# Adding the experts' outputs to token rows in DRAM, block by block, instead of gathering them after the last block

## The chip, the cores and the metric

The kernel runs on one core of one Trainium2 chip. The metric is the device time of one execution in microseconds. Five engines work side by side, each through its own list of instructions: TensorE (PE in the profile; PEld is its weight load), VectorE (DVE), ScalarE (ACT), GpSimd (POOL) and SyncE (SP). They meet through semaphores only. Transfers are issued by SP, ACT or POOL and carried out by 16 DMA engines that all of them share.

## The reference

The program is one step of a two-layer decoder trunk over 576 tokens (512 prompt tokens and 64 sample tokens), width 1024, float32. Each layer mixes tokens by three kinds of heads and then has a feed-forward part. That of layer 0 is dense; that of layer 1, to which the change belongs, is a mixture of 8 experts of which each token uses 2. Then comes the final norm:

```
def moe(x):
    logits = xf @ moe_router                      # 8 experts
    top_v, top_i = lax.top_k(logits, 2)
    gw = softmax(top_v)
    comb = sum(one_hot(top_i, 8) * gw[..., None], axis=1)
    for e in range(8):
        y = y + comb[:, e:e+1] * ((silu(xf @ w1[e]) * (xf @ w3[e])) @ w2[e])    # 1024 -> 1408 -> 1024
    return y

x = x + moe(rmsnorm(x, norm_ffn_w))
y = x * rsqrt(mean(x * x) + 1e-6) * norm_final_w
```

The whole step returns y for both groups of tokens and the new caches and states of the two layers.

## The kernel before, in words

Everything up to layer 1's experts keeps the activations with channels on the 128 partitions. For the experts this turns round: tokens lie on partitions, in five tiles (four of 128 tokens, one of 64), and `XT` (`xt_buf`) holds the rows of x before the experts, 1024 numbers a token.

**Routing.** DVE finds each token's two experts (`moe_choose_dve`). A token and one of its experts are a pair, and there are 1152 of them. Pairs of one expert get consecutive slots, and each expert's slots begin at a multiple of 128, so that 16 blocks (`NBK`) of 128 slots always do. PE sums over the tokens with two small products (`moe_count_pe`); DVE turns the sums into a slot for each pair (`slot_buf`), an expert for each block (`ebt_buf`) and a weight for each pair (`gain`). POOL then writes the normed rows to their slots in `d_xs` in DRAM with ten indirect transfers, two for each tile (`moe_scatter_pool`, L2248). Slots without a token hold zeros, which layer 0 wrote there in its feed-forward part (`ex_sp`).

**Blocks.** For each of the 16 blocks SP loads the block's 128 rows and the expert's weights, in 18 units of up to 1 MB, into a ring of 11 slots (`moe_sp`, L2308). It issues a unit as soon as PE is done with the one 11 places ahead. ACT casts each unit to the high half of a split product (L2412), up to four units ahead of PE. DVE computes the low half (L2456) and PE multiplies (L2334, L2338 up; L2365, L2371 down). The output of a block, 128 slots by 1024, stands in PSUM banks 6 and 7. ACT copies it to `yb_buf` (L2436) and issues its transfer to `d_ys` in DRAM (L2438).

**After the last block.** When all of `d_ys` is written, POOL gathers for every tile the rows of its tokens' two slots (`moe_gather_pool`, L2260, ten indirect transfers through two buffers). DVE adds them to XT, each times its weight (L2504 twice a tile), ACT squares and sums (L2518), DVE scales the mean (L2507), ACT takes the root (L2520), DVE the reciprocal (L2509) and the product with the norm's weights (L2510), and SP stores the tile (L2860). The order of all engines is the order of the code; `v(...)` and `a(...)` are a helper (L165) that makes an engine wait for each of its own instructions. In `fin_dve` the next tile's additions come after this tile's last product.

Of the kernel before, what the change touches and what calls it, by code (L numbers as in the profile page):

```python
# [8 lines left out]
I32 = mybir.dt.int32  # L9
# [178 lines left out]
def build(nc, A):  # L188

    with ExitStack() as ctx:  # L190
        sems = {}
        A["xs"] = nc.dram_tensor("d_xs", (NBK * P, D), F32).ap()
        A["ys"] = nc.dram_tensor("d_ys", (NBK * P, D), F32).ap()
# [84 lines left out]
        yg_buf = put_at("yg_buf", 4 * D, mc + 9216)  # L278
# [1806 lines left out]
        YG = yg_buf[:, :].rearrange("p (i c d) -> p i c d", i=2, c=2)  # L2085
# [26 lines left out]
        frs = rt.take(5)  # L2112

# [276 lines left out]
        def moe_act():  # L2390
# [29 lines left out]
            for b in range(NBK):  # L2420
# [76 lines left out]
        def fin_dve(v):  # L2497
            ve = nc.vector
            ve.wait_ge(S("moe_wfin"), 16)
            for i in range(5):  # L2500
                n = tok(i)
                ve.wait_ge(S(f"moe_yg_{i % 2}"), 32 * (i // 2 + 1))
                for k in range(2):
                    v(ve.scalar_tensor_tensor(XT[0:n, i, :], YG[0:n, i % 2, k, :], gain[0:n, k, i:i + 1], XT[0:n, i, :],  # L2504
                                              ALU.mult, ALU.add), *([S("moe_added")] if k else []))
                ve.wait_ge(S("moe_fsum"), i + 1)
                v(ve.tensor_scalar(frs[0:n, i:i + 1], fsum[0:n, i:i + 1], 1.0 / D, 1e-6, ALU.mult, ALU.add), S("moe_fmean"))  # L2507
                ve.wait_ge(S("moe_froot"), i + 1)
                v(ve.reciprocal(frs[0:n, i:i + 1], frs[0:n, i:i + 1]))  # L2509
                v(ve.scalar_tensor_tensor(XT[0:n, i, :], XT[0:n, i, :], frs[0:n, i:i + 1], WFIN[0:n, :], ALU.mult, ALU.mult),  # L2510
                  S("moe_fin"))

        def fin_act(a):
            ac = nc.scalar
            for i in range(5):
                n = tok(i)
                ac.wait_ge(S("moe_added"), i + 1)
                a(ac.activation(sq_buf[0:n, 0:D], XT[0:n, i, :], ACT.Square, accum_out=fsum[0:n, i:i + 1]), S("moe_fsum"))  # L2518
                ac.wait_ge(S("moe_fmean"), i + 1)
                a(ac.activation(frs[0:n, i:i + 1], frs[0:n, i:i + 1], ACT.Sqrt), S("moe_froot"))  # L2520
# [9 lines left out]
        def ex_sp(e):  # L2530
            for u in range(NUN):
# [99 lines left out]
        with nc.Block() as block:  # L2631
            @block.vector
            def _(eng):
# [20 lines left out]
                for l in range(DEPTH):  # L2654
# [77 lines left out]
            def _(eng):  # L2732
                for l in range(DEPTH):
# [9 lines left out]
                    else:  # L2743
                        moe_scatter_pool()
                        moe_gather_pool()

            @block.tensor
            def _(eng):
                eng.wait_ge(S("g_consts"), 16)
                eng.sem_inc(S("ex_unit_done"), FREE_PARTS)  # L2750
                for l in range(DEPTH):
# [23 lines left out]
                    else:  # L2775
                        moe_wo_pe()
                        moe_count_pe()
                        moe_pe()

            @block.sync  # L2780
            def _(eng):
# [4 lines left out]
                for l in range(DEPTH):  # L2786
# [63 lines left out]
                    if l == 0:  # L2850
# [3 lines left out]
                        eng.wait_ge(S("g_zero"), 16 * NBK)  # L2854
# [188 lines left out]
```

## Time and profile before

| | us |
|---|---|
| median of 3 runs | 2856.9 |
| lowest and highest run | 2844.24, 2858.02 |
| span of the profiled execution | 2850.7 |

The page gives no time of its own for the profiled execution beside its span. Its part on busy shares shows PE busy for 2468.7 us (87%), DVE for 1668.5 (59%), ACT for 1125.7 (39%) and POOL for 360.3 (13%). In the 40 equal slices of the span PE stands at 9 tenths from slice 30 to slice 39, which are the blocks, and DMA there too. PE stands at 3 in the last slice, in which the gathers and the final norm lie. A span runs from the first to the last instruction; a stretch in which PE has nothing to do is time that only the other engines and the transfers can shorten.

### The profile page before, as it was taken

Reading aid. Unit: us, or ns where it says so; the run is one execution under the profiler, and the core shown is the slowest. Engines: PE = TensorE matmul, PEld = TensorE weight load, DVE = VectorE, ACT = ScalarE, POOL = GpSimd, SP = SyncE. Lnnn points to the kernel's source line nnn. Section 1 sums busy time; section 2 is a strip of 40 time slices with the busy share of each in tenths; the row PEclk is TensorE's granted clock in tenths of the full one; section 3 lists DMA queues with packets and bytes.
Section 4 is the critical chain, followed back from the end, with each engine's and each line's share of the span. In section 5 each row is a group of like instructions: output and inputs, shape, how many; then the busy total and the mean of one; then the engine's idle time right before and its main releaser. Section 6 shows DMA issues by size and latency. Waiting matters only on the chain.

```text
span 2850.7 us, 39807 instructions
## 1 busy us (share of the span) xinstructions
PE 2468.7 (87%) x15802; PEld 2095.7 (74%) x15802; DVE 1668.5 (59%) x1990; ACT 1125.7 (39%) x1370; POOL 360.3 (13%) x160
## 2 busy tenths in 40 slices
PE   5996798698779999969977886979599999999993
PEld 5995686334779999969965863349488888888883
DVE  6853765524423122158627655243689898989895
ACT  4441000453222112134420004532577777777773
POOL 2330000000133333313310000002100000000001
PEclk9997888696889999989978986969799999999997
DMA  4220311300022343122203113001799999999993
GB/s 150 78 61 16 127 53 51 121 23 30 31 96 87 106 149 110 61 94 78 69 16 127 53 51 123 22 30 38 309 420 401 380 381 383 381 387 379 384 376 113
DMA packets 115995, 452.28 MB, mean 159 GB/s; under 512 B 12834, under 2 KB 47522, under 8 KB 86370
## 3 DMA queue, kind: packets, MB, share of 16 engines
q1 hardware_dynamic: 110882, 431.92, 41.3%
q0 software_dynamic: 2624, 9.44, 1.0%
q10 hardware_dynamic: 2304, 8.39, 0.7%
q8 instruction: 125, 2.05, 0.3%
q14 instruction: 60, 0.49, 0.1%
HBM read 415.00 MB, written 42.95 MB: 161 GB/s over the span
## 4 chain that ended last, share of the span: by engine, by line
PE 78%; DVE 12%; ACT 4%; issue 2%; DMA 2%; POOL 1%; another core or an unknown queue 1%; DVEq 0%; SPq 0%; ACTq 0%; POOLq 0%; PEldq 0%
PE ps_buf L508 31%; PE ps_buf L2334 12%; PE ps_buf L2338 6%; PE ps_buf L2365 6%; PE ps_buf L1161 3%; PE ps_buf L2371 3%; PE ps_buf L1196 2%; ACT arena L1735 2%; PE ps_buf L1651 2%; PE ps_buf L1685 1%; PE ps_buf L1149 1%; PE ps_buf L1838 1%; DVE h_buf L572 1%; PE ps_buf L2349 1%; DVE xl_buf L576 1%
## 5 line engine op out<-in xcount | busy, mean ns | idle before, releaser
L508 PE MATMUL ps_buf<-xh_buf,whl_buf 128*128 128x288 f32 x3648 | 663.2, 302 | 76.6 <-POOLq L165 40.5
L2456 DVE TENSOR_TENSOR ring_lo<-ring,high_buf 128x2048 fp32r<-128x2048 f32 (+2 forms) x288 | 594.4, 2108 | 51.7 <-ACT high_buf L2412 49.5
L508 PEld LDWEIGHTS ps_buf<-xh_buf,whl_buf 128*128 128x128 f32 x3648 | 549.6, 192 | 89.5 <-issue 65.0
L2412 ACT CAST high_buf<-ring 128x2048 fp32r<-128x2048 f32 (+2 forms) x288 | 503.0, 1764 | 127.2 <-PE ps_buf L2338 69.0
L508 PE MATMUL ps_buf<-xl_buf,whl_buf 128*128 128x288 f32 x1824 | 398.4, 300 | 0.0
L496 POOL TENSOR_TENSOR whl_buf<-arena,whl_buf 128x1024 fp32r<-128x1024 f32 (+1 forms) x114 | 294.1, 2579 | 602.1 <-ACTq L165 601.5
L493 ACT CAST whl_buf<-arena 128x1024 fp32r<-128x1024 f32 (+1 forms) x114 | 124.7, 1094 | 495.5 <-PE ps_buf L508 476.2
L508 PEld LDWEIGHTS ps_buf<-xl_buf,whl_buf 128*128 128x128 f32 x1824 | 299.0, 193 | 0.0
L2334 PE MATMUL ps_buf<-high_buf,xbh_buf 128*128 128x512 f32 (+1 forms) x768 | 289.8, 377 | 5.3 <-ACT high_buf L2412 5.3
L2334 PE MATMUL ps_buf<-high_buf,xbl_buf 128*128 128x512 f32 (+1 forms) x768 | 288.3, 375 | 0.0
L2338 PE MATMUL ps_buf<-ring_lo,xbh_buf 128*128 128x512 f32 (+1 forms) x768 | 196.1, 377 | 0.0
L2365 PE MATMUL ps_buf<-high_buf,ht_buf 128*128 128x512 f32 x704 | 181.2, 397 | 0.0
L496 POOL TENSOR_TENSOR whl_buf<-cols_buf,whl_buf 128x1024 fp32r<-128x1024 f32 x16 | 39.7, 2479 | 1005.3 <-ACTq L165 1004.9
L2334 PEld LDWEIGHTS ps_buf<-high_buf,xbh_buf 128*128 128x128 f32 x768 | 144.8, 189 | 28.6 <-issue 5.7
L2334 PEld LDWEIGHTS ps_buf<-high_buf,xbl_buf 128*128 128x128 f32 x768 | 144.7, 188 | 23.0
L2338 PEld LDWEIGHTS ps_buf<-ring_lo,xbh_buf 128*128 128x128 f32 x768 | 140.6, 188 | 24.8 <-DVE ring_lo L2456 3.3
L2365 PEld LDWEIGHTS ps_buf<-high_buf,ht_buf 128*128 128x128 f32 x704 | 129.8, 188 | 28.4
L2584 DVE TENSOR_TENSOR cols_buf<-arena,ps_buf 128x576 f32<-128x576 f32 x22 | 16.6, 755 | 212.2 <-PE ps_buf L508 212.2
L508 PE MATMUL ps_buf<-hh_buf,whl_buf 128*128 128x288 f32 x704 | 122.9, 296 | 0.0
L2260 POOL DMA_INDIRECT yg_buf<-d_ys,slot_buf x10 | 9.4, 936 | 805.5 <-DMA d_ys<-yb_buf 789.9
L508 PEld LDWEIGHTS ps_buf<-hh_buf,whl_buf 128*128 128x128 f32 x704 | 103.5, 188 | 0.0
L2371 PE MATMUL ps_buf<-ring_lo,ht_buf 128*128 128x512 f32 x352 | 97.7, 396 | 0.0
(519 smaller groups left out, 3395.8 us busy)
## 6 DMA issues: line engine op xcount, KB each, us to landing
ring<-d_moe_up SPq DMA_DIRECT2D x128, 1024.0 KB, 7.5
ring<-d_moe_dn SPq DMA_DIRECT2D x80, 1024.0 KB, 7.4
ring<-d_moe_up SPq DMA_DIRECT2D x64, 768.0 KB, 6.6
arena<-d_w_in SPq DMA_DIRECT2D x54, 512.0 KB, 3.6
arena<-d_w SPq DMA_DIRECT2D x44, 512.0 KB, 3.6
arena<-d_w SPq DMA_DIRECT2D x16, 704.0 KB, 4.0
arena<-d_pages_c SPq DMA_DIRECT2D x64, 128.0 KB, 2.1
cols_buf<-d_w_out SPq DMA_DIRECT2D x16, 512.0 KB, 3.6
```

Of the source, the lines that this page charges most:

```text
L493: a(nc.scalar.copy(part(slot, 0, nk, size), src), *sig)
L496: g(nc.gpsimd.tensor_tensor(part(slot, 1, nk, size), src, part(slot, 0, nk, size).bitcast(F32), ALU.subtract), *sig)
L508: last = nc.tensor.matmul(ps_buf[0:rows, b + a_, 0:HALF], w, m[:, a_ * HALF:(a_ + 1) * HALF], start=start, stop=stop)
L1161: last = pe.matmul(ps_buf[0:n, 3 * s_ + b, c], l_[0:n, c], r_[0:n, c], start=True, stop=True)
L1196: last = nc.tensor.matmul(bank(4 * j + 2 * g + half, 9 * 32 + 8), cw1[j][:, 8 * half + p_, :], ckb[:, :, j, g, 8 * p_:8 * p_ + 8], start=p ...
L1651: pe.matmul(ps_buf[:, b + g, at:at + n], cols[lo:lo + 64, keys(w), P * c:P * c + P], qrot[lo:lo + 64, h, P * c:SEQ], start=True, stop=False)
L2334: pe.matmul(ps_buf[:, o + w, 0:n], x_[:, b % 2, 4 * q + k, :], high_part(u)[:, n * k:n * k + n], start=q == 0 and k == 0 and i == 0, stop= ...
L2338: last = pe.matmul(ps_buf[:, o + w, 0:n], XBH[:, b % 2, 4 * q + k, :], low_part(u)[:, n * k:n * k + n], start=False, stop=q == 1 and k == 3)
L2365: pe.matmul(ps_buf[:, 6 + h, 0:512], t_[:, f, :], high_part(u)[:, c], start=f == 0 and i == 0, stop=False)
L2371: last = pe.matmul(ps_buf[:, 6 + h, 0:512], HTH[:, f, :], low_part(u)[:, c], start=False, stop=f == FC - 1)
L2412: ac.copy(high_part(n), ring[:, 2048 * slot:2048 * slot + unit_cols(n % BLOCK_UNITS)])\
L2456: ve.tensor_tensor(low_part(n), ring[:, at:at + unit_cols(n % BLOCK_UNITS)], high_part(n).bitcast(F32), ALU.subtract).then_inc(S("moe_lo"), 1)
```

## The change

Each block's rows are multiplied by their slots' weights on the way out of PSUM, and added to their tokens' rows in DRAM at once.

- A new DRAM tensor `d_ya` of 704 rows takes the place of `d_ys`. SP copies XT into its rows 0 to 575 (five transfers) before the first block. Rows 576 to 703 take what slots without a token would add; they are zeroed once in layer 0.
- `moe_who_dve` and `moe_who_pe` compute, for each slot, its token's row (`who_buf`) and its weight (`share_buf`). DVE makes ten one-hot matrices, and PE sums ten small products into PSUM bank 2. Two more small products ahead of `moe_count_pe` give rows of numbers to compare with.
- ACT's copy of a block's output becomes a product with `share_buf`, and ACT issues no transfer any more. POOL issues an indirect transfer that adds (`moe_add_pool`), one for each block. Each waits for the block's output and for the addition before it. ACT waits for the addition of two blocks ago before it writes `yb_buf` again.
- After the last addition SP loads the five tiles of `d_ya` back into XT. `fin_dve` has no additions left, and the norm's steps of two tiles overlap: the mean of tile i stands ahead of the reciprocal and the product of tile i-1, and on ACT the squares of tile i stand ahead of the root of tile i-1. The table for the root is loaded ahead of the first tile.

```diff
-        A["ys"] = nc.dram_tensor("d_ys", (NBK * P, D), F32).ap()
+        A["ya"] = nc.dram_tensor("d_ya", (T + P, D), F32).ap()
...
+        def moe_who_dve(v):
+            ve = nc.vector
+            blk = tb("blocks")[:, ::8]
+            wide_b = blk.unsqueeze(1).to_broadcast([P, 10, NBK])
+            flat_s = slots.rearrange("p k i -> p (k i)")
+            v(ve.tensor_scalar(at_blk, flat_s, 1.0 / P, -1.0 / P, ALU.mult, ALU.add))
+            v(ve.tensor_tensor(eq, at_blk.unsqueeze(2).to_broadcast([P, 10, NBK]), wide_b, ALU.is_ge))
+            v(ve.tensor_reduce(at_blk, eq, AX.X, ALU.add))
+            v(ve.tensor_scalar(at_blk, at_blk, -1.0, None, ALU.add))
+            v(ve.tensor_tensor(eq, at_blk.unsqueeze(2).to_broadcast([P, 10, NBK]), wide_b, ALU.is_equal))
+            v(ve.scalar_tensor_tensor(at_blk, at_blk, -float(P), flat_s, ALU.mult, ALU.add))
+            v(ve.tensor_copy(number, ps_buf[:, 1, 128:129]))
+            v(ve.tensor_scalar(tok5, tb("steps")[:, ::8], number, None, ALU.add))
+            v(ve.tensor_scalar(number, number, float(T), None, ALU.add))
+            for k in range(2):
+                ks = slice(5 * k, 5 * k + 5)
+                v(ve.tensor_tensor(AG[:, ks, 0, :], eq[:, ks, :], tok5.unsqueeze(2).to_broadcast([P, 5, NBK]), ALU.mult))
+            v(ve.tensor_tensor(AG[:, :, 1, :], eq, gain.rearrange("p k i -> p (k i)").unsqueeze(2).to_broadcast([P, 10, NBK]),
+                               ALU.mult))
+            for j in range(10):
+                if j >= 2:
+                    ve.wait_ge(S("moe_whose"), j - 1)
+                v(ve.tensor_scalar(OH[:, j % 2, :], ps_buf[:, 1, 0:P], at_blk[:, j:j + 1], None, ALU.is_equal), S("moe_oh"))
+            ve.wait_ge(S("moe_whose"), 10)
+            v(ve.tensor_copy(share_buf[:, :], ps_buf[:, 2, NBK:2 * NBK]))
...
+            v(ve.tensor_scalar(who_buf[:, :], eq[:, 0, :], -1.0, None, ALU.add), S("moe_who"))
+
+        def moe_who_pe():
+            pe = nc.tensor
+            for j in range(10):
+                n = tok(j % 5)
+                pe.wait_ge(S("moe_oh"), j + 1)
+                pe.matmul(ps_buf[:, 2, 0:2 * NBK], OH[0:n, j % 2, :], AG[0:n, j].rearrange("p w b -> p (w b)"),
+                          start=j == 0, stop=j == 9).then_inc(S("moe_whose"), 1)
...
-        def moe_gather_pool():
...
+        def moe_add_pool():
+            g = nc.gpsimd
+            g.wait_ge(S("moe_ya"), 16 * 5)
+            g.wait_ge(S("moe_who"), 1)
+            for b in range(NBK):
+                g.wait_ge(S("moe_y"), b + 1)
+                if b:
+                    g.wait_ge(S("moe_acc"), 16 * b)
+                g.indirect_dma_start(A["ya"], bass.IndirectOffsetOnAxis(ap=who_buf[:, b:b + 1], axis=0), YB[:, b % 2, :], None,
+                                     compute_op=ALU.add).then_inc(S("moe_acc"), 16)
...
+            sp.wait_ge(S("moe_xt"), KD)
+            for i, (t0, n) in enumerate(TILES):
+                sp.dma_start(A["ya"][t0:t0 + n], XT[0:n, i, :]).then_inc(S("moe_ya"), 16)
             sp.wait_ge(S("moe_experts"), 1)
...
+                if b == 0:
+                    ac.wait_ge(S("moe_who"), 1)
                 if b >= 2:
-                    ac.wait_ge(S(f"moe_ys_{b % 2}"), 16 * (b // 2))
-                ac.copy(YB[:, b % 2, :].rearrange("p (h c) -> p h c", h=2), ps_buf[:, 6:8, 0:512]).then_inc(S("moe_y"), 1)
-                ac.wait_ge(S("moe_y"), b + 1)
-                ac.dma_start(A["ys"][P * b:P * b + P], YB[:, b % 2, :]).then_inc(S(f"moe_ys_{b % 2}"), 16)
+                    ac.wait_ge(S("moe_acc"), 16 * (b - 1))
+                ac.mul(YB[:, b % 2, :].rearrange("p (h c) -> p h c", h=2), ps_buf[:, 6:8, 0:512], share_buf[:, b:b + 1])\
+                    .then_inc(S("moe_y"), 1)
...
+            for i in range(6):
+                if i < 5:
+                    n = tok(i)
+                    ve.wait_ge(S("moe_fsum"), i + 1)
+                    v(ve.tensor_scalar(frs[0:n, i:i + 1], fsum[0:n, i:i + 1], 1.0 / D, 1e-6, ALU.mult, ALU.add), S("moe_fmean"))
+                if i:
+                    n = tok(i - 1)
+                    ve.wait_ge(S("moe_froot"), i)
+                    v(ve.reciprocal(frs[0:n, i - 1:i], frs[0:n, i - 1:i]))
+                    v(ve.scalar_tensor_tensor(XT[0:n, i - 1, :], XT[0:n, i - 1, :], frs[0:n, i - 1:i], WFIN[0:n, :],
+                                              ALU.mult, ALU.mult), S("moe_fin"))
...
+                eng.wait_ge(S("moe_acc"), 16 * NBK)
+                for i, (t0, n) in enumerate(TILES):
+                    eng.dma_start(XT[0:n, i, :], A["ya"][t0:t0 + n]).then_inc(S(f"moe_back_{i}"), 16)
```

How the instructions stand on an engine is shown here at three places, before and now. The line numbers are those of each kernel's own file, `part_...` and `ex_...` are semaphores that several stages share, and a row with xN stands for N alike.

POOL before, from the last scatters to the end: `d_xs` is the slots' input, `yg_buf` the gathered rows.

```order
L2248 DMA d_xs<-xn_tok,slot_buf 2048x1024 [waits part_75]
L2248 DMA d_xs<-xn_tok,slot_buf 2048x1024
L2260 DMA yg_buf<-d_ys,slot_buf 128x1024 [waits part_90,part_89]
L2260 DMA yg_buf<-d_ys,slot_buf 128x1024 x3
L2260 DMA yg_buf<-d_ys,slot_buf 128x1024 [waits part_54]
L2260 DMA yg_buf<-d_ys,slot_buf 128x1024
```

POOL now, the same place to the end of its list:

```order
L2296 DMA d_xs<-xn_tok,slot_buf 2048x1024 [waits part_75]
L2296 DMA d_xs<-xn_tok,slot_buf 2048x1024
L2307 DMA d_ya<-yb_buf,who_buf 704x1024 [waits part_88,ex_raw_in_0,part_97]
L2307 DMA d_ya<-yb_buf,who_buf 704x1024 [waits part_89,part_88] x15
L2686 UNCONDITIONAL_BRANCH
```

The ten gathers behind the blocks are gone; sixteen additions stand among the blocks, and the last of them behind the last block.

DVE now, between the routing and the first block (before, the product into `xbt_buf` followed at once on the third of these rows):

```order
L2238 TENSOR_SCALAR mo_buf<-mo_buf 128x5 [waits dve_chain,ex_silu]
L2239 RECIPROCAL mo_buf<-mo_buf 128x5 [waits dve_chain]
L2240 TENSOR_TENSOR mo_buf<-mo_buf 128x5 [waits dve_chain]
L2247 TENSOR_SCALAR mo_buf<-mo_buf 128x10 [waits dve_chain]
L2248 TENSOR_TENSOR mo_buf<-mo_buf,tab 128x160 [waits dve_chain]
L2249 TENSOR_REDUCE mo_buf<-mo_buf 128x10 [waits dve_chain]
```

and the end of the piece that is new there:

```order
L2264 TENSOR_SCALAR oh_buf<-ps_buf,mo_buf 128x128 [waits dve_chain] x2
L2264 TENSOR_SCALAR oh_buf<-ps_buf,mo_buf 128x128 [waits dve_chain,ex_raw_in_1] x8
L2266 COPY share_buf<-ps_buf 128x16 [waits dve_chain,ex_raw_in_1]
L2267 TENSOR_SCALAR mo_buf<-ps_buf,mo_buf 128x16 [waits dve_chain]
L2268 TENSOR_TENSOR mo_buf<-mo_buf,ps_buf 128x16 [waits dve_chain]
L2269 TENSOR_SCALAR who_buf<-mo_buf 128x16 [waits dve_chain]
L2498 TENSOR_TENSOR xbt_buf<-ps_buf,small 128x1024 [waits dve_chain,ex_raw_free]
```

Twenty-six instructions now stand ahead of the first block's product on DVE, eight of them with a wait for PE.

DVE before, in the final norm, the first tile and the start of the second:

```order
L2504 SCALAR_TENSOR_TENSOR xt_buf<-yg_buf,mo_buf,xt_buf 128x1024 [waits part_53,part_52]
L2504 SCALAR_TENSOR_TENSOR xt_buf<-yg_buf,mo_buf,xt_buf 128x1024 [waits dve_chain]
L2507 TENSOR_SCALAR mo_buf<-mo_buf 128x1 [waits dve_chain,part_55]
L2509 RECIPROCAL mo_buf<-mo_buf 128x1 [waits dve_chain,part_57]
L2510 SCALAR_TENSOR_TENSOR xt_buf<-xt_buf,mo_buf,wbc_buf 128x1024 [waits dve_chain]
L2504 SCALAR_TENSOR_TENSOR xt_buf<-yg_buf,mo_buf,xt_buf 128x1024 [waits dve_chain,part_59]
```

DVE now:

```order
L2554 TENSOR_SCALAR mo_buf<-mo_buf 128x1 [waits part_56,part_55]
L2554 TENSOR_SCALAR mo_buf<-mo_buf 128x1 [waits dve_chain,part_56]
L2558 RECIPROCAL mo_buf<-mo_buf 128x1 [waits dve_chain,part_58]
L2559 SCALAR_TENSOR_TENSOR xt_buf<-xt_buf,mo_buf,wbc_buf 128x1024 [waits dve_chain]
L2554 TENSOR_SCALAR mo_buf<-mo_buf 128x1 [waits dve_chain,part_56]
L2558 RECIPROCAL mo_buf<-mo_buf 128x1 [waits dve_chain,part_58]
```

The two additions of a tile are gone, and the mean of the next tile stands ahead of this tile's reciprocal.

## Rows read from the trace of the kernel before

**Rows 1.** The page: its first line.
```profile
span 2850.7 us, 39807 instructions
```

**Rows 2.** Busy time of each engine by stretch: two blocks and the end.
```profile
core 0: us, PE busy (x) PEld busy (x) DVE busy (x) ACT busy (x) POOL busy (x), PEclk, DMA share, GB/s
...
2083.00:2131.00 48.00, 48.00 (x230) 40.58 (x229) 43.36 (x27) 34.97 (x26) 0.00 (x0) 1.00 1.02 420
...
2276.00:2324.00 48.00, 48.00 (x230) 40.59 (x229) 43.30 (x28) 34.97 (x26) 0.00 (x0) 1.00 0.99 382
...
2805.00:2851.00 46.00, 0.00 (x0) 0.00 (x0) 20.82 (x25) 8.89 (x17) 9.36 (x10) 0.54 0.48 165
```

**Rows 3.** Waits from 2035 to 2805: total us, times, longest; SP's queue apart.
```profile
ACT high_buf L2412 <- DMA ring<-d_moe_up: 3.9, 6, 1.2
...
SPq L2308 <- PE ps_buf L2338: 382.3, 187, 6.0
SPq L2308 <- PE ps_buf L2371: 209.7, 90, 3.6
```

**Rows 4.** Transfers issued in 2083:2131 and then 2276:2324: count, KB, us to landing.
```profile
ring<-d_moe_up SPq DMA_DIRECT2D x8, 1024.0 KB, 13.0
...
ring<-d_moe_up SPq DMA_DIRECT2D x8, 1024.0 KB, 6.6
```

**Rows 5.** Chain that ended last, from 2803: start us, us, what.
```profile
2804.84 1.02 ACT yb_buf L2436
...
2808.50 0.74 issue
...
2810.52 5.37 DMA yg_buf<-d_ys,slot_buf
...
2829.23 1.29 DVE xt_buf L2504
...
2835.30 1.30 DVE xt_buf L2504
...
2846.00 1.28 DVE xt_buf L2510
```

**Rows 6.** Timeline of the third tile's norm: start us, us, instruction, idle before.
```profile
2831.92 1.06 ACT L2518 ACTIVATE sq_buf<-xt_buf 128x1024 f32<-128x1024 f32 x1 [4.40 <-DVEq L165]
...
2833.15 0.15 DVE L2507 TENSOR_SCALAR mo_buf<-mo_buf 128x1 f32<-128x1 f32 x1 [1.32 <-ACTq L165]
...
2833.39 0.20 ACT L2520 ACTIVATE mo_buf<-mo_buf 128x1 f32<-128x1 f32 x1 [0.32 <-DVEq L165]
2833.67 0.16 DVE L2509 RECIPROCAL mo_buf<-mo_buf 128x1 f32<-128x1 f32 x1 [0.37 <-ACTq L165]
2833.87 1.28 DVE L2510 SCALAR_TENSOR_TENSOR xt_buf<-xt_buf,mo_buf,wbc_buf 128x1024 f32<-128x1024 f32 x1
```

**Rows 7.** By tile, xn_tok: scatters, ACT's scaling, landing; then xb_buf's landing.
```profile
L2248 POOL DMA_INDIRECT d_xs<-xn_tok,slot_buf x10: 896/952/1132, 2007.0 to 2018.5; - x10
L2163 ACT ACTIVATE xn_tok<-xt_buf,mo_buf x5: 1147/1147/1148, 1999.1 to 2004.2; 128x1024 f32<-128x1024 f32 x4, 64x1024 f32<-64x1024 f32 x1
...
DMA to landing us min/median/max: 3.5/4.4/5.2
...
DMA to landing us min/median/max: 3.2/5.9/16.0
```

**Rows 8.** Chain from the routing to the first block, and two waits there.
```profile
2002.32 0.65 PE ps_buf L2237 x2
...
2003.43 0.21 DVE mo_buf L2208
...
2033.88 3.73 PE ps_buf L2334 x8
...
PE ps_buf L2317 <- DMA xb_buf<-d_xs: 23.2, 1, 23.2
DVE xbt_buf L2448 <- PE ps_buf L2317: 20.1, 1, 20.1
```

More of the change, by code:

```diff
@@ L277, in build @@
         xt_buf = put_at("xt_buf", 5 * D, mc + 4096)
-        yg_buf = put_at("yg_buf", 4 * D, mc + 9216)
+        who_buf = put_at("who_buf", NBK, mr + RING * 2048, I32)
+        share_buf = put_at("share_buf", NBK, mr + RING * 2048 + NBK)
+        ag_buf = put_at("ag_buf", 10 * 2 * NBK, mr + RING * 2048 + 2 * NBK)
+        oh_buf = put_at("oh_buf", 2 * P, mc + 3840)
         wbc_buf = put_at("wbc_buf", D, mc + 13312)
@@ L2084, in build @@
         YB = grid(yb_buf, 0, 2, D)
-        YG = yg_buf[:, :].rearrange("p (i c d) -> p i c d", i=2, c=2)
+        AG = ag_buf[:, :].rearrange("p (j w b) -> p j w b", j=10, w=2)
+        OH = grid(oh_buf, 0, 2, P)
         WFIN = wbc_buf[:, 0:D]
@@ L2112, in build @@
         frs = rt.take(5)
+        at_blk = rt.take(10)
+        eq = rt.take(10, NBK)
+        tok5 = rt.take(5)
+        number = rt.take(1)
         def tok(i):
@@ L2232, in moe_choose_dve @@
             v(ve.tensor_tensor(gain[:, 1, :], diff, gain[:, 0, :], ALU.mult))
+        def moe_who_dve(v):
[23 more added lines that the diff above has]
+            v(ve.tensor_copy(share_buf[:, :], ps_buf[:, 2, NBK:2 * NBK]))
+            v(ve.tensor_scalar(eq[:, 0, :], ps_buf[:, 2, 0:NBK], 0.5, number, ALU.is_lt, ALU.mult))
+            v(ve.tensor_tensor(eq[:, 0, :], eq[:, 0, :], ps_buf[:, 2, 0:NBK], ALU.add))
+            v(ve.tensor_scalar(who_buf[:, :], eq[:, 0, :], -1.0, None, ALU.add), S("moe_who"))
@@ L2234, in moe_count_pe @@
+        def moe_who_pe():
[5 more added lines that the diff above has]
+                          start=j == 0, stop=j == 9).then_inc(S("moe_whose"), 1)
         def moe_count_pe():
             pe = nc.tensor
+            pe.wait_ge(S("wo_out"), KD)
+            pe.matmul(ps_buf[:, 1, 0:P], tb("ones"), tb("rwp")[:, P:2 * P], start=True, stop=True)
+            pe.matmul(ps_buf[:, 1, 128:129], tb("rwp")[:, P:2 * P], tb("ones")[:, 0:1], start=True, stop=True)
@@ L2242, in moe_scatter_pool @@
             g.wait_ge(S("moe_slots"), 1)
-            g.wait_ge(S("g_zero"), 16 * NBK)
+            g.wait_ge(S("g_zero"), 16 * (NBK + 1))
             for i in range(5):
@@ L2499, in fin_dve @@
             ve.wait_ge(S("moe_wfin"), 16)
[L2500 to L2511, printed above, removed]
+            for i in range(6):
[9 more added lines that the diff above has]
+                                              ALU.mult, ALU.mult), S("moe_fin"))
@@ L2513, in fin_act @@
         def fin_act(a):
             ac = nc.scalar
[L2515 to L2520, printed above, removed]
+            a(ac.activation(diff, rstd_t, ACT.Sqrt))
+            for i in range(6):
+                if i < 5:
+                    n = tok(i)
+                    ac.wait_ge(S(f"moe_back_{i}"), 16)
+                    a(ac.activation(sq_buf[0:n, 0:D], XT[0:n, i, :], ACT.Square, accum_out=fsum[0:n, i:i + 1]), S("moe_fsum"))
+                if i:
+                    n = tok(i - 1)
+                    ac.wait_ge(S("moe_fmean"), i)
+                    a(ac.activation(frs[0:n, i - 1:i], frs[0:n, i - 1:i], ACT.Sqrt), S("moe_froot"))
@@ L2536, in ex_sp @@
                     sync.dma_start(A["xs"][P * u:P * u + P], zero_buf).then_inc(S("g_zero"), 16)
+                if e == 1 and u == NBK:
+                    sync.dma_start(A["ya"][T:T + P], zero_buf).then_inc(S("g_zero"), 16)
         def ex_act(a, e):
@@ L2692, in _ @@
                         moe_choose_dve(v)
+                        moe_who_dve(v)
                         moe_dve(v)
@@ L2744, in _ @@
                         moe_scatter_pool()
-                        moe_gather_pool()
+                        moe_add_pool()
             @block.tensor
@@ L2777, in _ @@
                         moe_count_pe()
+                        moe_who_pe()
                         moe_pe()
```

12 lines of the change are left out of this document (1 added, 11 removed).

## The prediction

> **What bounds the kernel now.** The page's first line gives the execution that I work on: a span of 2850.7 us [rows 1]. It lists no time outside the span. The span is 6.2 us below the median of the three runs (2856.9) and between the lowest and the highest (2844.24, 2858.02). I sum against the span and take the difference off the median.
>
> I read the stretches first. In the blocks PE is busy in all of the 48 us of each row, at a granted clock of 1.00, while POOL does nothing; in the last 46 us PE does nothing and DVE 20.8 us [rows 2]. So PE sets the pace in the blocks and the chain behind them is bare. Sixteen blocks run from 2033.88 [rows 8] to ACT's copy at 2804.84 [rows 5]: 771.0 us, 48.2 a block.
>
> Then the waits between 2035 and 2805. ACT waited 3.9 us for weights in all; SP waited 592 us (382.3 + 209.7) for PE to free a ring slot [rows 3]. So transfers are ahead of PE. By how much? DMA moves 420 GB/s where it has a backlog (2083:2131, a load takes 13.0 us to land) and 382 where it has none (6.6 us) [rows 2, 4]. A load is issued when PE finishes the unit 11 ahead, and ACT wants it 4 ahead: 7 units of 48.2/18 = 2.68 us, so 18.7 us. The margin is 5.7 us in the early blocks, 12 later. A block at 382 GB/s leaves 48.2 x (1 - 382/420) = 4.4 us of the DMA engines unused.
>
> Last the chain at the end: copy 1.02, a transfer, 0.74 until POOL starts, gathers (5.37 from the second one's start), and then the tiles one behind another. A tile takes 2835.30 - 2829.23 = 6.07 us; the last product starts at 2846.00, 1.28 long, and 3.4 us later (the last store) the span ends [rows 5]. Per tile DVE works 2 x 1.29 for the additions and 1.59 for the rest, and idles while ACT squares and takes the root [rows 5, 6].
>
> **The change part by part.**
>
> *The end* is where the time lies, from 2804.84 on.
> - ACT's product in place of the copy: between 1.01 (the copy) and 1.15 (ACT's scaling of as many elements from SBUF [rows 7]); I take 1.06, to 2805.9.
> - POOL starts after the output, with no transfer between. The one hand-over shown took 0.74 [rows 5], and it followed a transfer and two waits. I take 0.6, between 0.3 and 0.74: 2806.5.
> - The adding transfer, 512 KB, alone in the queues. No row shows one. The nearest is a scatter of the same rows to DRAM, 3.5 us to land at best and 4.4 in the middle, with others beside it [rows 7]. An addition must also read the rows. Lower bound 3.5 (the read overlaps). Upper bound 9.8: a gather in the shape of 5.37 [rows 5] and a scatter of 4.4 one after the other. I take 5.5, nearest to the idle scatter plus one more pass over the data and its latency: 2812.0.
> - SP loads the tiles back. A 512 KB load from DRAM landed in 3.2 at best [rows 7], and 512 KB at 420 GB/s is 1.25, so I let the tiles arrive 1.25 apart: first 2815.2, second 2816.5, the fifth by 2819.9. (If all five shared the engines evenly: first near 2819.)
> - The norm. Square to mean is 1.23 (2831.92 to 2833.15) [rows 6]: first sum at 2816.4, second at 2817.7. Then root (0.20 and about 0.1 of hand-over) 2818.0, reciprocal to 2818.2, product to 2819.5. From there DVE has 0.15 + 0.16 + 1.28 a tile [rows 6] and three steps of its own chain of about 0.04: 1.71. ACT has 1.23 + 0.26, less. So DVE paces it: 4 x 1.71, less the last tile's missing mean, 2826.1. The table load for the root (one is in the tail before) lies beside the addition and costs nothing.
> - The last store as before, 3.4: the span ends at 2829.5.
>
> 2850.7 - 2829.5 = 21.2 us saved. Of these, 4 x (6.07 - 1.71) = 17.4 come from the shorter step from tile to tile, and 3.8 from the way to the first tile's product, where a store and gathers give place to an addition and a load.
>
> *The blocks.* Per block the 0.52 MB store goes (1.25 us of the engines at 420 GB/s) and an adding transfer of the same size comes. Let it take X us of the engines. Below, X = 1.25: no change. Above, 9.8, if it held all the engines from issue to landing as bounded above. The nearest row is the scatters': ten were issued 1.25 us apart (2007.0 to 2018.5 [rows 7]) and landed in 4.4, so each took about 1.25. With one more read I take 2.5. Cover: 4.4 + 1.25 = 5.6 us a block before DMA falls behind, so 2.5 costs nothing. PE, ACT and DVE do the same work, and ACT is rid of issuing a transfer. POOL issues behind a wait for the previous addition, 48 us ago; behind that wait only further additions are queued, and ACT needs one two blocks old. Also nothing.
>
> The Trainium skill (Collectives: The Full Stack, The bandwidth ceiling: the fold count and why AG ≠ RS ≠ AR) says that an add in the DMA engines costs no cycles itself but needs two source reads and one write. By that rule X would be 2.5 at most; the trace of before has no adding transfer to hold it against.
>
> *Before the blocks.* DVE gets 26 instructions. It stood idle for 20.1 us ahead of the first block's product, and PE for 23.2 [rows 8]. Twelve small ones and four final ones at about 0.25, four wider ones at up to 0.4: 5 us with the chain. Ten one-hots: at least 0.3 each; at most one round trip through PE each, which took 1.11 us from PE's start to DVE's start for four products [rows 8]. So 3 to 11 us, in all 8 to 16, within 20.1, and PE ends under a microsecond later than DVE. If that cover were gone, each microsecond would be one of the span. SP's five copies of XT are issued before it waits for the routing, and POOL's scatters come later. PE's two number products stand ahead of the count products, where PE waits for DVE, and are fewer than the four that took 1.11. The extra zeroing is one more transfer in layer 0 beside 16 alike.
>
> What is not covered: POOL's ten scatters lie on the chain to the first block. The first, which ran while DVE was still busy, took 1.13 us, the middle one 0.95 [rows 7]. Now DVE is busy beside all of them. Between 0 and 10 x 0.18 = 1.8 us; since the transfers themselves need 1.25 us each and POOL's step is just that long, I take 0.5.
> The Trainium skill (DMA: Bandwidth & Descriptors, SWDGE vs HWDGE vs iDMA) says that GpSimd writes its descriptors into SBUF rings, from which some DVE modes lock it out. By that rule the 1.8 would be the value, and more if DVE ran such a mode throughout. The 1.132 beside 0.952 is in agreement with it, though one instruction shows little.
>
> Sum: 21.2 - 0.5 = 20.7 saved. 2856.9 - 20.7 = 2836.2 us.
>
> **The rivals.**
> 1. *The adding transfer holds the DMA engines in the blocks.* Place: ring loads in blocks 1 to 15. It decides from X = 5.6 on; each us above costs 15, less the 5.7 of margin used once. With X = 9 that is 3.4 x 15 - 5.7 = 45 lost; 2836.2 + 45 = 2881, slower than before. It breaks even near X = 7.4. For it: DMA share already 0.99 to 1.02 [rows 2]. Against it: SP's 592 us of waits for PE [rows 3], and that the scatters, made by the same engine's descriptors, ran at full rate [rows 7].
> 2. *The last addition is slow only in itself*: rows of an engine are read and written one after another, but other queues pass. Then it takes its upper 9.8 or a little more, 13: 2836.2 + 7.5 = 2843.7. For it: none of the rows shows a read and a write of the same place. Against it: blocks would not show it.
> 3. *The loads back arrive together*, not 1.25 apart: first tile at 2819.0 and not 2815.2. 2836.2 + 3.8 = 2840. For it: five loads, one queue, 16 engines. Against it: in a backlog ring loads take 13.0 us each [rows 4], yet PE gets one every 2.68, so they land one after another.
> 4. *The change does not do what it says*, and the one-hot work delays the first block: from 20.1 us on. At 25 us it would cost 5: 2841.
>
> **How the numbers follow.** A measurement of this kernel can tell about 0.5%, 14.3 us; under 2842.6 is faster. Forecast 0.66, most of it faster (0.57), the rest (0.09) within, since the runs of before alone are 14 us apart. Rival 3: 0.08 (0.06 faster). Rival 2: 0.12 (0.04 faster, 0.08 within). Rival 4: 0.03 (0.01, 0.02). Rival 1: 0.11 (0.01 within; 0.10 slower). Together faster 0.68, within 0.22, slower 0.10. The forecast's own range is 2829 to 2847: a landing of 3.5 in place of 5.5, a quicker norm and a low run below; a landing of 9.8, the 1.8 of the scatters and a high run above. With rivals 2 to 4 and the start of rival 1 the range is 2828 to 2856. It leaves out most of rival 1.
>
> **What would show it.** In the blocks: PE still 48.0 of 48, and ACT's waits for the ring near 3.9 us; landing of ring loads over 18 us and PE idle would be rival 1. At the end: from PE's last product to the span's end 25 us, not 46; a `yb_buf` to `d_ya` landing of 5.5 (9 and more is rival 2); first square 10.4 us after ACT's product; products of the norm 1.7 apart. Before the blocks: first block's product at the same distance from the routing within 2 us, DVE idle 4 to 12 us ahead of it. The prediction is wrong if the time is above 2842.6.

## The result, and the profile after

Over eight runs of each kernel the median went from 2851.42 to 2832.12 us: a ratio of 0.9935, 95% interval 0.9913 to 0.9958. The forecast was 2836.2, which is 20.7 saved; 19.3 were. The runs of one kernel lie some 26 us apart (2821.56 to 2847.5), so what follows compares stretches of single executions, not whole spans.

The profiled execution of the changed kernel, its page's first line:
```profile
span 2833.4 us, 39897 instructions
```
That is 17.3 us less than [rows 1]. Three stretches make it up. The tail, from the start of ACT's last output to the span's end, was 2850.7 - 2804.84 = 45.9 and is 2833.4 - 2806.24 = 27.2: 18.7 saved. The blocks, from PE's first product to that output, take 771.0 in both. From the slots (DVE's `slot_buf`, 2006.52 and 2007.62) to PE's first product it was 27.4 and is 27.6. The remaining 1.1 us lie ahead of the slots, in code that the change doesn't touch.

Busy time by stretch, answering to [rows 2]:
```profile
core 0: us, PE busy (x) PEld busy (x) DVE busy (x) ACT busy (x) POOL busy (x), PEclk, DMA share, GB/s
2083.00:2131.00 48.00, 48.00 (x231) 40.55 (x230) 43.32 (x27) 35.05 (x25) 3.25 (x1) 1.00 1.02 410
2276.00:2324.00 48.00, 48.00 (x230) 40.55 (x230) 43.34 (x28) 35.08 (x25) 1.56 (x1) 1.00 1.00 387
2805.00:2833.00 28.00, 1.20 (x6) 0.63 (x4) 7.98 (x15) 9.36 (x18) 1.55 (x1) 0.59 0.59 188
```
In the blocks PE is busy in all of the 48 us, as before; POOL is new there. In the tail (a window of 28 us, against one of 46 before) DVE works 8.0 us and not 20.8: the two additions of 1.29 a tile are gone.

DMA queues (packets, MB, share of the 16 engines) and landings of what was issued, 2276 to 2324, answering to the second half of [rows 4]:
```profile
q0 software_dynamic: 144, 0.52, 6.5%
...
ring<-d_moe_up SPq DMA_DIRECT2D x8, 1024.0 KB, 7.5
...
d_ya<-yb_buf,who_buf POOLq DMA_INDIRECT x1, 10.6
```
6.5% of 48 us is 3.1 us of all 16 engines: this is what the prediction called X. Ring loads land in 7.5 us and not 6.6. ACT still hardly waits for them from 2040 to 2795 (engine, line, releaser: total us, times, longest), against [rows 3]:
```profile
ACT high_buf L2461 <- DMA ring<-d_moe_up: 3.0, 5, 0.6
```

The tail as a timeline (start us, us, instruction, idle before and its releaser):
```profile
2806.24 1.11 ACT L2487 ACTIVATE yb_buf<-ps_buf,share_buf 128x1024 f32<-128x1024 f32 x1 [6.52 <-PE ps_buf L2420]
...
2807.63 1.55 POOL L2307 DMA_INDIRECT d_ya<-yb_buf,who_buf  x1 [41.27 <-ACT yb_buf L2487]
...
2813.75 2.34 SPq L2917 DMA_DIRECT2D xt_buf<-d_ya  x5
2817.16 1.06 ACT L2569 ACTIVATE sq_buf<-xt_buf 128x1024 f32<-128x1024 f32 x1 [8.29 <-DMA xt_buf<-d_ya]
...
2820.18 1.28 DVE L2559 SCALAR_TENSOR_TENSOR xt_buf<-xt_buf,mo_buf,wbc_buf 128x1024 f32<-128x1024 f32 x1
2821.49 1.06 ACT L2569 ACTIVATE sq_buf<-xt_buf 128x1024 f32<-128x1024 f32 x1 [1.59 <-DMA xt_buf<-d_ya]
...
2823.24 1.29 DVE L2559 SCALAR_TENSOR_TENSOR xt_buf<-xt_buf,mo_buf,wbc_buf 128x1024 f32<-128x1024 f32 x1
2823.37 1.06 ACT L2569 ACTIVATE sq_buf<-xt_buf 128x1024 f32<-128x1024 f32 x1 [0.40 <-DMA xt_buf<-d_ya]
...
2825.17 1.28 DVE L2559 SCALAR_TENSOR_TENSOR xt_buf<-xt_buf,mo_buf,wbc_buf 128x1024 f32<-128x1024 f32 x1
...
2826.61 0.15 DVE L2554 TENSOR_SCALAR mo_buf<-mo_buf 64x1 f32<-64x1 f32 x1
...
2826.90 0.16 DVE L2558 RECIPROCAL mo_buf<-mo_buf 128x1 f32<-128x1 f32 x1
2827.10 1.28 DVE L2559 SCALAR_TENSOR_TENSOR xt_buf<-xt_buf,mo_buf,wbc_buf 128x1024 f32<-128x1024 f32 x1
...
2828.72 1.28 DVE L2559 SCALAR_TENSOR_TENSOR xt_buf<-xt_buf,mo_buf,wbc_buf 64x1024 f32<-64x1024 f32 x1
```
Three things stand out. The addition runs from 2807.63 to 2813.75, when SP may issue the loads: 6.1 us. The third and fourth squares wait 1.59 and 0.40 us for their tiles, so from the third on the tiles come late. On ACT the square of the third tile stands ahead of the root of the second, so the second tile's product (2823.24) waits for the third tile's load. And the last product starts 22.5 us after ACT's output where 20.0 were forecast, which is all of the tail's 2.5 us of excess.

### The profile page after: what moved, and what is told of

The parts are those of the page before. It is cut to its first block, busy times and chain, and to the rows that moved or that the text cites. A ratio compares the mean times of both kernels' runs of the same rounds, so it can differ in the third digit from the quotient of the medians.

```text
span 2833.4 us, 39897 instructions
## 1 busy us (share of the span) xinstructions
PE 2479.3 (88%) x15826; PEld 2104.8 (74%) x15826; DVE 1663.5 (59%) x2006; ACT 1125.8 (40%) x1371; POOL 386.8 (14%) x166
## 4 chain that ended last, share of the span: by engine, by line
PE 77%; DVE 11%; ACT 4%; issue 3%; DMA 2%; POOL 1%; another core or an unknown queue 1%; SPq 0%; DVEq 0%; ACTq 0%; POOLq 0%; PEldq 0%
PE ps_buf L511 31%; PE ps_buf L2383 11%; PE ps_buf L2387 5%; PE ps_buf L2414 5%; PE ps_buf L1164 3%; PE ps_buf L2420 3%; PE ps_buf L1199 2%; ACT arena L1738 2%; PE ps_buf L1654 2%; PE ps_buf L1688 1%; PE ps_buf L1152 1%; PE ps_buf L1841 1%; DVE h_buf L575 1%; DMA d_ya<-yb_buf,who_buf 1%; PE ps_buf L2398 1%
## 5 line engine op out<-in xcount | busy, mean ns | idle before, releaser
L2307 POOL DMA_INDIRECT d_ya<-yb_buf,who_buf x16 | 34.5, 2155 | 754.2 <-ACT yb_buf L2487 754.2
```

## Experiments

Two theories stood at first. A, the prediction's: the tail gains from the additions' leaving DVE, the blocks hide the adding transfers because X is under 5.6 us. B: the overlapped norm alone brings most of it. Each ratio is to the kernel before, on the same chip. "Tail" and "blocks" are the stretches defined above.

**norm_only**: the kernel before, with a tile's reciprocal and product put behind the additions of the next tile. Only DVE's loop is changed, shown here cut; ACT still squares a tile and takes its root before the next one's square:
```diff
-            for i in range(5):
+            for i in range(6):
+                if i < 5:
                     ve.wait_ge(S(f"moe_yg_{i % 2}"), 32 * (i // 2 + 1))
                     ...
+                if i:
+                    ve.wait_ge(S("moe_froot"), i)
+                    ...
+                if i < 5:
                     ve.wait_ge(S("moe_fsum"), i + 1)
                     ...
-                ve.wait_ge(S("moe_froot"), i + 1)
-                ...
```


> The kernel before with its gathers and its store to d_ys, and only the final norm reordered: a tile's reciprocal and product come behind the next tile's two additions. Theory A (additions by DVE were the larger part of the tail's tile step, their removal gives most of the gain): a step needs 2 x 1.29 for the additions and 1.6 for the rest on DVE, 4.3 to 4.6 us in place of 6.07, so 6 to 7 us saved: ratio to before 0.9975 to 0.998, tail from ACT's last copy to the span's end 39 to 40 us in place of 45.9. Theory B (the overlap of the norm is what gives the gain of the change): 12 us or more saved, tail under 34 us.

Measured: 0.9989 (0.9970 to 1.0009), the tail 41.8 us where it was 45.9. Part of its timeline:
```profile
2824.59 1.28 DVE L2511 SCALAR_TENSOR_TENSOR xt_buf<-xt_buf,mo_buf,wbc_buf 128x1024 f32<-128x1024 f32 x1
...
2826.81 2.61 DVE L2505 SCALAR_TENSOR_TENSOR xt_buf<-yg_buf,mo_buf,xt_buf 128x1024 f32<-128x1024 f32 x2 [0.64 <-DMA yg_buf<-d_ys,slot_buf]
...
2833.14 2.60 DVE L2505 SCALAR_TENSOR_TENSOR xt_buf<-yg_buf,mo_buf,xt_buf 128x1024 f32<-128x1024 f32 x2 [1.79 <-DMA yg_buf<-d_ys,slot_buf]
...
2842.90 1.28 DVE L2511 SCALAR_TENSOR_TENSOR xt_buf<-xt_buf,mo_buf,wbc_buf 64x1024 f32<-64x1024 f32 x1
```
The reordering saves 4.1 us of the tail, less than the 6 to 7 expected, and the median doesn't show it (the interval holds 1). The four steps from the first product to the last shrink from 24.3 us to 18.3 (2842.90 - 2824.59). That is the saving expected, although the gathers, with buffers for two tiles only, became a new wait (0.64, then 1.79 us). But the first product starts 18.75 us after ACT's copy and not 16.88 (2821.72 in the kernel before), since the second tile's additions now stand ahead of it: 1.9 us go back. B, which wanted 12 us or more, falls.

**add_only**: the changed kernel with the norm's tiles one behind another, as before.
```diff
-            for i in range(6):
-                if i < 5:
+            for i in range(5):
                     ve.wait_ge(S("moe_fsum"), i + 1)
                     ...
-                if i:
-                    ve.wait_ge(S("moe_froot"), i)
+                ve.wait_ge(S("moe_froot"), i + 1)
                     ...
```


> The changed kernel with the old order in the final norm: mean, reciprocal and product of one tile before the next, the same on ACT. Theory A: with no additions left on DVE the squares of the next tile run beside the product anyway, so a step is 0.15 + 0.3 + 0.17 + 1.29 + hand-overs = 2.0 to 2.1 us against 1.7, and the loads hide a part: 0.5 to 1.5 us longer than the changed kernel, tail 27.7 to 28.7 us against 27.2, ratio to before 0.993 to 0.995. Theory B: at least 8 us longer than the changed kernel, tail over 35 us.

Measured: 0.9935 (0.9913 to 0.9957), the tail 2842.2 - 2815.84 = 26.4 us, no longer than the 27.2 with the overlap, where 27.7 to 28.7 were expected.
```profile
2817.22 1.55 POOL L2307 DMA_INDIRECT d_ya<-yb_buf,who_buf  x1 [41.27 <-ACT yb_buf L2487]
...
2823.21 2.30 SPq L2911 DMA_DIRECT2D xt_buf<-d_ya  x5
...
2828.56 1.28 DVE L2556 SCALAR_TENSOR_TENSOR xt_buf<-xt_buf,mo_buf,wbc_buf 128x1024 f32<-128x1024 f32 x1
...
2837.55 1.28 DVE L2556 SCALAR_TENSOR_TENSOR xt_buf<-xt_buf,mo_buf,wbc_buf 64x1024 f32<-64x1024 f32 x1
```
The first product starts 5.35 us after SP's load (2828.56 - 2823.21), against 6.43 in the changed kernel (2820.18 - 2813.75): the overlap puts the second square ahead of the first root on ACT. The four steps after it take 8.99 us here and 8.54 there. So the overlap gives 0.45 and takes 1.1: beside the addition in DRAM the pipelined norm is worth nothing. The gain is the addition's, but for one part that both kernels have: the root's table, 1.28 us to load, stands in the first tile's chain before (its root starts 1.33 us after the mean, those of the other tiles 0.25) and beside the addition now. By these rows that is 1.1 us; no run tried it alone.

**plain_scatter**: the changed kernel with the addition taken out of the transfer.
```diff
-    ... YB[:, b % 2, :], None, compute_op=ALU.add)
+    ... YB[:, b % 2, :], None)
```


> The changed kernel with plain indirect writes in place of the adding ones: the sum over a token's two experts and x is left out (the last write stands). It prices the addition. If an addition costs a second read of the rows in the engines, the software queue's share in a block falls from 6.5% of 48 us (3.1 us for 0.52 MB) to about 2.7% (1.3 us), the last transfer lands in 3.5 to 4.5 us in place of 6.1, and the tail is 2 us shorter, 25 us. If the 3.1 and 6.1 us belong to the indirect form and not to the addition: share and landing unchanged. In both cases PE stays busy in all of each 48 us.

What is left out is the sum: of all that is written to a row the last stands.

Measured: 0.9938 (0.9913 to 0.9962), the tail 23.8 us (25 expected). Its rows by tile and its queue from 2570 to 2618, then the changed kernel's rows by tile:
```profile
L2307 POOL DMA_INDIRECT d_ya<-yb_buf,who_buf x16: 949/949/2789, 2080.5 to 2798.8; - x16
...
DMA to landing us min/median/max: 3.3/8.0/11.5
...
q0 software_dynamic: 144, 0.52, 2.7%
```
```profile
L2307 POOL DMA_INDIRECT d_ya<-yb_buf,who_buf x16: 1553/1568/3618, 2089.3 to 2807.6; - x16
...
DMA to landing us min/median/max: 6.1/10.0/14.5
```
The addition costs 0.6 us of POOL's instruction (1.57 against 0.95), 2.8 us of landing alone in the queues (6.1 against 3.3), and 3.1 against 1.3 us of the DMA engines (6.5% against 2.7% of 48 us; the changed kernel's queue has 6.5% from 2570 to 2618 too). The tail is 3.3 us shorter without it; the median doesn't tell the two apart. The third and fourth squares wait for their loads here too (0.68 and 1.00), so those waits don't come from the addition.

**two_queues**: tiles 1 and 3 are loaded back by ACT's queue, the others by SP's.
```diff
+            for i in (1, 3):
+                ac.dma_start(XT[:, i, :], A["ya"][TILES[i][0]:TILES[i][0] + P]).then_inc(...)
```


> The changed kernel with the loads of tiles 1 and 3 back into SBUF issued by ACT and the others by SP. In the changed kernel tile 2 landed 3.06 us behind tile 1 and tile 3 another 1.9, and ACT waited 1.6 + 0.4 us for them. If one queue's order or issue is what delays them: tiles arrive 1.3 apart, no such waits, tail shorter by 1.5 to 2 us (25.2 to 25.7). If the 16 engines share the transfers with some of them late: arrivals the same within 0.5 us for the last tile, tail 27.2 within 0.5; the first tile may come later, since it shares the engines with tile 1 from the start.

Measured: 0.9939 (0.9914 to 0.9965), the tail 26.7 us.
```profile
2803.59 1.34 SPq L2921 DMA_DIRECT2D xt_buf<-d_ya  x3
2803.65 0.83 ACTq L2567 DMA_DIRECT2D xt_buf<-d_ya  x2
2807.67 1.06 ACT L2572 ACTIVATE sq_buf<-xt_buf 128x1024 f32<-128x1024 f32 x1 [8.86 <-DMA xt_buf<-d_ya]
...
2810.78 1.06 ACT L2572 ACTIVATE sq_buf<-xt_buf 128x1024 f32<-128x1024 f32 x1 [0.37 <-DMA xt_buf<-d_ya]
...
2812.62 1.28 DVE L2559 SCALAR_TENSOR_TENSOR xt_buf<-xt_buf,mo_buf,wbc_buf 128x1024 f32<-128x1024 f32 x1
...
2814.56 1.28 DVE L2559 SCALAR_TENSOR_TENSOR xt_buf<-xt_buf,mo_buf,wbc_buf 128x1024 f32<-128x1024 f32 x1
```
The first tile comes 0.7 us later (4.08 after the load's issue, where it was 3.41), the third square waits 0.37 and not 1.59. Most of that is the later start: counted from the loads' issue the third square starts at 7.2 us here and at 7.7 in the changed kernel. The fourth waits for no load any more. In all the second queue gains 0.4 us, so the expectation of 1.5 to 2 fails and that of 27.2 within 0.5 holds: the one queue holds the later tiles back by little. The products now start 1.93 us apart (2810.69, 2812.62, 2814.56), and behind the third square no load is waited for, so 1.93 is DVE's own step.

**adds_twice** and **adds_thrice**: POOL issues the addition of each block but the last two or three times, which doubles or triples X; the output then holds those blocks two or three times.
```diff
-                g.indirect_dma_start(A["ya"], ..., compute_op=ALU.add)
+                for again in range(2 if b < NBK - 1 else 1):   # 3 in adds_thrice
+                    if m:
+                        g.wait_ge(S("moe_acc"), 16 * m)
+                    g.indirect_dma_start(A["ya"], ..., compute_op=ALU.add)
+                    m += 1
```


> The changed kernel with every block but the last added twice, the second time when the first has landed; the output holds those blocks twice. It sizes the cover of the additions. Theory A (engines): an addition holds the DMA engines for 3.1 us by its queue's share (6.5% of 48 us) and 5.6 us a block are free. Two hold 6.2: about 0.6 us too much a block, which the ring's margin of 5.7 us and more takes up: PE still busy in all of each 48 us, ring loads landing later than 7.5 us in the median (9 to 12), time as the changed kernel within 5 us. Theory B (no shared resource, the landing of 10 us is latency alone): ring loads' landing unchanged at 7.5.

Measured: 0.9923 (0.9906 to 0.9941), the blocks 2802.85 - 2031.17 = 771.7 us. Stretch, queue and landing, 2276 to 2324:
```profile
2276.00:2324.00 48.00, 48.00 (x231) 40.70 (x229) 43.34 (x27) 34.95 (x26) 4.12 (x2) 1.00 1.02 399
```
```profile
q0 software_dynamic: 288, 1.05, 10.9%
...
ring<-d_moe_up SPq DMA_DIRECT2D x8, 1024.0 KB, 12.6
```
Two additions take 10.9% of 48, 5.2 us, just under the 5.6 of cover. Nothing is lost; the ring's loads land late (12.6 us), under the 18.7 after which ACT would wait. That they land later at all (7.5 in the changed kernel, 9 to 12 expected) speaks for a shared resource.

> The same with three additions for every block but the last. Theory A: 9.3 us of the engines a block, 3.7 more than are free; over 15 blocks 55 us, less the margin used once: 40 to 55 us longer than the changed kernel, ratio to before 1.007 to 1.013, the blocks from first product to ACT's last output 810 to 826 us in place of 771, and ACT waiting for ring loads. Theory B: as the changed kernel, ratio 0.9935 within 0.003, blocks 771 us.

Measured: 1.0001 (0.9983 to 1.0018), the blocks 2818.22 - 2026.10 = 792.1 us, 21 more. The same rows, and ACT's waits over the blocks:
```profile
2276.00:2324.00 48.00, 47.03 (x224) 39.48 (x223) 42.24 (x28) 33.70 (x25) 7.22 (x3) 1.00 1.02 389
```
```profile
q0 software_dynamic: 432, 1.57, 16.4%
...
ring<-d_moe_up SPq DMA_DIRECT2D x8, 1024.0 KB, 24.0
```
```profile
ACT high_buf L2464 <- DMA ring<-d_moe_up: 107.7, 126, 3.1
ACT high_buf L2464 <- DMA ring<-d_moe_dn: 66.9, 54, 3.5
```
Two of ACT's outputs of a block, twelve blocks apart:
```profile
2126.42 1.11 ACT L2490 ACTIVATE yb_buf<-ps_buf,share_buf 128x1024 f32<-128x1024 f32 x1
...
2725.72 1.10 ACT L2490 ACTIVATE yb_buf<-ps_buf,share_buf 128x1024 f32<-128x1024 f32 x1
```
Here rival 1 is real: the ring lands in 24.0 us, past 18.7; ACT waits 175 us in all, and PE falls to 47.0 of 48. Three additions take 16.4% of 48, 7.9 us, so one takes 2.6, as in adds_twice; the 40 to 55 expected came from 3.1. By the prediction's sum 2.3 over the cover makes 2.3 x 15 = 34, less the margin of 5.7 that it used once 29; 21 were lost. The blocks show where it errs. The first two outputs of ACT lie 48.1 us apart, as in the changed kernel; from the second on they lie 49.9 apart ((2725.72 - 2126.42) / 12), which is 1.8 a block and not 2.3. The cover was a little larger than 5.6: about 6.1 by these two numbers, an estimate. And where it begins fits the margin: loads issued from 2080 to 2126 landed in 18.2 us, under 18.7, and those from 2126 to 2176 in 20.3.

**last_by_pe**: the last block isn't added in DRAM. SP loads the tiles back while it is still computed, and PE adds its rows through products with one-hot matrices (`OC`) into PSUM, from which DVE adds them to the tiles.
```diff
-            for b in range(NBK):
+            for b in range(NBK - 1):
...
+            for i in range(5):
+                for h in range(2):
+                    pe.matmul(ps_buf[0:n, ...], OC[:, i, 0:n], YB[:, (NBK - 1) % 2, 512 * h:512 * h + 512])
...
+                v(ve.tensor_tensor(XT[0:n, i, :], XT[0:n, i, :], ps_buf[0:n, ...], ALU.add))
```


> The changed kernel with the last block not added in DRAM: the sum over the first 15 blocks is loaded back into SBUF during the last block, and PE multiplies the last block's weighted output by one-hot matrices of slot to token (made beside the others), for each tile of tokens two products of 128x512 in float32 into PSUM, which DVE adds; the adding transfer's 6.1 us and the first load's 3.4 leave the tail. If the tail is what its chain shows: product of ACT 1.1, first PE product about 2, then DVE at 1.29 + 1.6 + hand-overs = 3.05 us a tile with the first addition at 3.2, and 3.4 for the last store: tail 22 to 24 us against 27.2, blocks 771 us as before, ratio to before 0.9915 to 0.993. Rival: PE's float32 products are slower than 1.5 us a half tile and pace the tiles, tail 27 us or more, no gain.

Measured: 0.9910 (0.9888 to 0.9932), the tail 2828.4 - 2804.22 = 24.2 us, just over the 22 to 24 expected.
```profile
2804.22 1.11 ACT L2504 ACTIVATE yb_buf<-ps_buf,share_buf 128x1024 f32<-128x1024 f32 x1 [6.52 <-PE ps_buf L2427]
...
2805.39 8.99 PE L2452 MATMUL ps_buf<-yb_buf,oc_buf 128*128 128x512 f32 x20 [1.20 <-ACT yb_buf L2504]
...
2807.51 1.22 DVE L2572 TENSOR_TENSOR xt_buf<-xt_buf,ps_buf 128x1024 f32<-128x1024 f32 x1 [7.29 <-PE ps_buf L2452]
...
2812.51 1.28 DVE L2585 SCALAR_TENSOR_TENSOR xt_buf<-xt_buf,mo_buf,wbc_buf 128x1024 f32<-128x1024 f32 x1
...
2815.89 1.28 DVE L2585 SCALAR_TENSOR_TENSOR xt_buf<-xt_buf,mo_buf,wbc_buf 128x1024 f32<-128x1024 f32 x1
```
The first product starts 8.3 us after ACT's output (13.9 in the changed kernel). The next two steps take 3.38 and 3.36, since DVE has an addition of 1.22 in each of them again, and the last two, without one, 2.16 and 2.27: 11.2 in all against 8.5. It beats the kernel before clearly. Against the changed kernel it is shown by the tail alone, 3.0 us shorter; the medians come from separate sessions and their intervals overlap.

## Why the prediction was right

*The tail* was forecast at 24.7 us and took 27.2. By its steps:
- ACT's product was 1.11 (forecast 1.06), and POOL started 0.28 after it (0.6). That the transfer no longer stands between them was right.
- The last addition landed in 6.1, forecast 5.5, bounds 3.5 and 9.8. plain_scatter shows what it is made of: 3.3 for the scatter, 2.8 for the addition. Rival 2, 9.8 and more, is out.
- First tile 3.4 after the load's issue, forecast 3.2; from its square to the first product 3.0, as forecast.
- The four steps between products were forecast at 1.71, 6.6 in all, and took 8.54: 3.06, 1.93, 1.93 and 1.62. This is the term that was mis-sized, in two places. The 1.93 is DVE's own step, as two_queues shows where no load is late. The forecast allowed about 0.04 us for each of three hand-overs between DVE's own instructions. Only that from reciprocal to product is so short; from a product to the next mean it is 0.16 (2825.17 + 1.28 to 2826.61) and from the mean to the reciprocal 0.14, though ACT had its sum ready at 2826.1 and its root at 2826.4. The first of the two stood in the rows of before: 2835.30 - (2833.87 + 1.28) = 0.15 [rows 5, 6]. This makes 0.8 of the 1.9.
- The other 1.1 is in the 3.06: the third tile wasn't there in time, and through the order on ACT the second tile's product waited for it. Rival 3 foresaw a late first tile and 3.8 us. The first came on time, so what cost 1.1 is another thing than that rival: a late third.

The sum of the differences is 0.6 up to the first product and 1.9 behind it. The tail's saving, 18.7, came mostly from where the prediction put it: before, the last product started 41.2 us after ACT's output, of which 4 x 6.07 (24.3) were steps; now it starts after 22.5, of which 8.5 are steps. 15.7 of the 18.7 are the shorter steps, the rest the shorter way to the first, of which the table's load is 1.1. The reason given was right for the additions: their leaving DVE does it. The overlap, on which the step of 1.71 was counted, gives nothing (add_only).

*The blocks* were forecast at no cost, from X = 2.5 and a cover of 5.6. X is 3.1 by its share, and the blocks took 771.0. adds_twice (5.2 us, nothing lost) and adds_thrice (7.9 us, 21 lost) enclose the forecast's limit, and the break-even that it put near 7.4 lies close to adds_thrice, whose median equals that of the kernel before. X = 2.5 was twice a plain scatter. The addition takes 2.4 times the engines' time of plain_scatter (6.5% against 2.7%) where it runs alone, and 2.0 times (2.6 us against 1.3) where two or three run in a block. The Trainium skill (Collectives: The Full Stack, The bandwidth ceiling: the fold count and why AG ≠ RS ≠ AR) has two source reads and one write for an add, from which the prediction had its twofold. The 2.0 agree with that and the 2.4 are more; no run here splits them into reads and write. Its other part, that it isn't the cycles of the add that cost, can't be told from these runs either: the shares hold all of it.

*Before the blocks* 0.5 us were forecast, and the stretch is 0.2 longer. DVE's added work took from 2009.70 to 2020.27, 10.6 us (forecast 8 to 16), and waits and scatters stand so:
```profile
DVE xbt_buf L2498 <- PE ps_buf L2366: 9.4, 1, 9.4
PE ps_buf L2366 <- DMA xb_buf<-d_xs: 8.3, 1, 8.3
```
```profile
L2296 POOL DMA_INDIRECT d_xs<-xn_tok,slot_buf x10: 895/961/1129, 2008.1 to 2019.7; - x10
```
DVE is still idle for 9.4 us ahead of the first block (20.1 in [rows 8]), so rival 4 was far off. The scatters' middle went from 0.952 to 0.961 us with DVE busy beside them, not to 1.13. The prediction had read the slow first scatter as the work of a busy DVE. In the changed kernel too only the first takes 1.13, and the next, with DVE just as busy, 0.98 and less: by these rows the 1.13 belongs to being first. The Trainium skill (DMA: Bandwidth & Descriptors, SWDGE vs HWDGE vs iDMA) has some DVE modes lock GpSimd out of its descriptor rings. These DVE instructions did not, by this row; whether others would, no run here shows.

That the median came 4.1 us under the forecast, while the profiled tail was 2.5 over it, has to do with the base: the forecast stood on the median of three runs, 2856.9; that of eight was 2851.42. So the absolute time is nearer than the parts deserve; the 20.7 against 19.3 saved is the fairer comparison.

## What to carry to other kernels

Where a reduction waits at the end for all of its inputs, adding each part in DRAM as it is made moves the work under the compute: here 24 us of steps became 8.5. Ask first how much of the DMA engines a stage leaves free (bytes moved against the rate in a backlog, and how far ahead of use loads are issued), and price an adding transfer at 2 to 2.4 plain ones. Read the hand-overs between an engine's own instructions from the trace as well: they were 0.8 of the 1.9 us that the steps were off by here. After such a move look at the end again: an overlap that saved 4 us of the tail before saved nothing after, and the last part may be cheaper by another way than the one that suits the rest.

## What was not expected of the hardware

- An accumulating indirect transfer of 512 KB costs POOL 1.57 us where a plain one costs 0.95, and 3.1 us of the engines (2.6 where two or three run in a block) where that costs 1.3.
- Five loads issued together by one queue into idle engines don't arrive evenly: the first two squares followed on one another, and the third waited 1.6 us for its tile. It wasn't the rate. By 2821.0 the engines had moved 2.24 of the five tiles' 2.36 MB, and from there to 2822.4 they were busy for 27%; the third tile landed at 2821.5 and the fourth at 2823.3. The tiles waited for a few last packets. Two queues moved this about (tail 0.4 us shorter). Why those packets are late stays open.
- Executions differ ahead of the slots, not behind them. In the nine profiled executions DVE's `slot_buf` started between 1997.8 and 2017.5 us, and from it to ACT's last output it took 798.2 to 799.2 us in every kernel but adds_thrice (819.5). The mean granted clock goes with the time (0.908 in the run of 2821.56, 0.897 in that of 2847.5), but which makes which isn't shown. What makes the earlier part vary wasn't tried.
